# First attention of a two-block model laid out features by tokens, two heads per step, with its gates by tanh

## The reference, cut to what matters

```python
def first_block(x, ...):
    h = rms_norm(x, norm_mix_g[i])
    za_u, za_v, q, k, v_att, g_a, g_b = jnp.split(h @ w_in[i], offsets, axis=-1)   # 7 parts of 1024
    y_a = sgu_mixer(gelu(za_u), gelu(za_v), w_s, b_s, ln_g, ln_b)   # u * (tril(W_s) v + b) per chunk of 128 tokens
    y_b = moba_attention(heads(q), heads(k), heads(v_att), rel_bias)  # 16 heads of 64, causal over 256 tokens
    merged = jax.nn.sigmoid(g_a) * y_a + jax.nn.sigmoid(g_b) * y_b
    x = x + merged @ w_out[i]
    h = rms_norm(x, norm_ffn_g[i])
    x = x + jnp.square(jax.nn.relu(h @ w_ff1[i])) @ w_ff2[i]
    ...
```

## Time and profile before

| | us |
|---|---|
| median of 3 runs | 1606.94 (1603.93 to 1608.2) |
| profiled execution: its time, its span | 1607.9, 1605.6 |
| PE busy | 1497.6 (93%) |
| DVE busy, ACT busy | 554.0 (35%), 466.3 (29%) |

### The profile page before, as it was taken

How to read it: one execution, slowest core, us unless ns; L and a number is a source line. 1 busy time by engine, 2 the same in 40 slices (tenths; PEclk the granted TensorE clock), 3 DMA queues, 4 the chain that set the end, 5 groups by cost and what they waited for, 6 DMA issues and landing times.

```text
span 1605.6 us, 20677 instructions
## 1 busy us (share of the span) xinstructions
PE 1497.6 (93%) x7963; PEld 931.0 (58%) x7963; DVE 554.0 (35%) x862; ACT 466.3 (29%) x785; POOL 37.0 (2%) x42
## 2 busy tenths in 40 slices
PE   7999979999999999979999989889889899999996
PEld 6897869988889987744434324324334343444342
DVE  5754566654574767641111101101101111111112
ACT  5535635452463676321111101101101111111111
POOL 1000000000020000120000000000000000000000
PEclk9999989999999999899999999999999999999999
DMA  8464334545544321779999999999999999999996
GB/s 303 162 212 156 105 125 158 195 173 183 187 155 158 106 105 53 285 300 422 417 414 422 421 422 422 422 422 422 422 421 423 422 422 404 411 421 422 422 421 251
DMA packets 106930, 489.27 MB, mean 305 GB/s; under 512 B 9391, under 2 KB 11571, under 8 KB 60020
## 3 DMA queue, kind: packets, MB, share of 16 engines
q1 hardware_dynamic: 105604, 484.16, 76.0%
q0 software_dynamic: 1184, 4.26, 0.8%
q10 hardware_dynamic: 80, 0.02, 0.0%
HBM read 506.21 MB, written 1.08 MB: 316 GB/s over the span
## 4 chain that ended last, share of the span: by engine, by line
PE 55%; DMA 23%; DVE 5%; ACT 2%; issue 1%; SPq 1%; DVEq 0%; ACTq 0%
PE bank L980 20%; DMA slots<-in_w_up_dram 20%; PE bank L1419 18%; PE bank L1454 8%; DMA slots<-in_w_down_dram 3%; PE bank L1369 3%; PE bank L1379 2%; DVE w_split L1556 1%; ACT w_split L606 1%; SPq L435 1%; PE bank L970 1%; PE bank L1042 1%; DVE xeT L2067 0%; ACT h_hi L596 0%; PE bank L1050 0%
## 5 line engine op out<-in xcount | busy, mean ns | idle before, releaser
L1419 PE MATMUL bank<-slots,xeT 128*64 128x512 f32 x1536 | 354.7, 616 | 41.0 <-DMA slots<-in_w_up_dram 38.6
L1419 PEld LDWEIGHTS bank<-slots,xeT 128*64 128x64 f32 x1536 | 112.6, 141 | 278.5 <-issue 219.2
L1454 PE MATMUL bank<-slots,heT 128*64 128x512 f32 x1024 | 227.2, 595 | 9.5 <-ACT heT L909 7.5
L1556 DVE TENSOR_TENSOR w_split<-raw,w_split 128x2048 fp32r<-128x2048 f32 (+2 forms) x96 | 205.6, 2170 | 77.8 <-ACT w_split L606 77.6
L980 PE MATMUL bank<-w_split,h_hi 128*128 128x512 f32 (+1 forms) x672 | 211.6, 398 | 6.8 <-DVE h_lo L1546 3.9
L980 PE MATMUL bank<-h_hi,w_split 128*128 128x256 f32 x1120 | 208.0, 286 | 2.2 <-DVE w_split L1556 2.2
L606 ACT ACTIVATE w_split<-raw 128x2048 fp32r<-128x2048 f32 (+2 forms) x96 | 170.9, 1816 | 63.0 <-PE bank L980 56.4
L980 PEld LDWEIGHTS bank<-h_hi,w_split 128*128 128x128 f32 x1120 | 177.6, 194 | 3.8 <-DVE w_split L1556 2.6
L2076 DVE TENSOR_TENSOR h_e<-bank,h_e 128x512 f32<-128x512 f32 x32 | 22.1, 692 | 423.7 <-PE bank L1419 423.7
L980 PE MATMUL bank<-h_lo,w_split 128*128 128x256 f32 x560 | 159.5, 285 | 0.0
L1454 PEld LDWEIGHTS bank<-slots,heT 128*64 128x64 f32 x1024 | 70.7, 137 | 147.4 <-issue 130.1
(11 more groups left out here) (329 smaller groups left out, 1391.0 us busy)
## 6 DMA issues: line engine op xcount, KB each, us to landing
slots<-in_w_up_dram SPq DMA_DIRECT2D x128, 1024.0 KB
slots<-in_w_down_dram SPq DMA_DIRECT2D x128, 1024.0 KB
areas<-in_w_gate_dram SPq DMA_DIRECT2D x64, 1024.0 KB, 19.4
slots<-in_w_gate_dram SPq DMA_DIRECT2D x64, 1024.0 KB
raw<-in_w_in_dram SPq DMA_DIRECT2D x42, 1024.0 KB, 5.2
raw<-in_w_ff_dram SPq DMA_DIRECT2D x32, 1024.0 KB, 5.2
raw<-in_w_out_dram SPq DMA_DIRECT2D x12, 1024.0 KB, 5.0
raw<-in_w_ple_gate_dram SPq DMA_DIRECT2D x4, 1024.0 KB, 5.2
```

The lines of the kernel that those rows point to most:

```text
L1419: last = mm(bank[SLOTS * e:SLOTS * e + SLOTS, :], xeT[:, k, odd, SLOTS * e:SLOTS * e + SLOTS], expert_panel(w, e, odd)[:, k, :], start=(k ...
L1454: last = mm(banks[half][SLOTS * e:SLOTS * e + SLOTS, :], heT[:, c, SLOTS * e:SLOTS * e + SLOTS], expert_panel("down", e, odd)[:, c, 512 * ...
L1556: last = tt(lo, source, hi, ALU.subtract)
```

## The change

The gates, `u`, the attention's output and their merge are kept features by tokens, as q and k are. So the panels u, gb and ga take the column form; the SGU mix has `v_rows` as its stationary operand and gives features by tokens, its bias coming as a row broadcast over the partitions (`b_row`, a new DMA of 128x1024 behind the layer norm's two, and the small one of `b_sgu` is gone). A step holds the two heads of a 128-feature tile. The probabilities are scaled by DVE ahead of their transposes (`head_norm`), and the values matmuls have the 64 columns of `va` as stationary operand, write the two halves of bank 7's partitions, and give the transposed output; so `turn(T_MERGED)` goes. The sigmoids become `tanh(x/2)`, with the factor 0.5 applied as the merged tiles are rounded, and merging happens in three pieces (`merge`, `round_merged`, `split_merged`). The first three quarters of wo panel 0 move in among the last heads. In the diff the first loop over `KT` is ACT's, the second DVE's.

```diff
-           ("va", 0), ("va", 1), ("gb", 0), ("gb", 1), ("ga", 0), ("ga", 1), ("wo", 0), ("wo", 1)]
+           ("va", 0), ("va", 1), ("gb", 0), ("ga", 0), ("gb", 1), ("ga", 1), ("wo", 0), ("wo", 1)]
...
+                    sp.dma_start(b_row.rearrange("p g t -> p (g t)"),
+                                 b_sgu.rearrange("a g t -> a (g t)").to_broadcast([P, D])).then_inc(ln_loaded, 16)
...
-            pool.wait_ge(merged, MT)
+            pool.wait_ge(scores_taken, HEADS)
...
-                        ins = act_({"ga": sga, "gb": sgb}[kind][:, b, half], bank[:, :], ACT.Sigmoid)
+                        dst = {"ga": sgaT, "gb": sgbT}[kind][:, tiles, :]
+                        ins = act_(dst.rearrange("p k t -> p (k t)"), bank[:, :], ACT.Tanh, scale=0.5)
...
+            for j in range(KT):
+                if j:
+                    pair_turned(j - 1)
+                if j % 2:
+                    empty(*(("gb", 0), ("ga", 0), ("gb", 1), ("ga", 1))[j // 2])
+                head_exp(2 * j)
+                head_exp(2 * j + 1)
+                for q in SPLIT_BESIDE[j]:
+                    split(2 * AT["ga", 0] + q)
+                if j == 4:
+                    round_merged(1, 0, 4, 2)
+                if j == 7:
+                    round_merged(2, 4, 6, 1)
...
-                if kind in ("q", "k", "q2", "ff1", "xbc"):
+                if kind in ("u", "q", "k", "ga", "gb", "q2", "ff1", "xbc"):
...
+            def score_pair(j):
+
+                if j:
+                    pe.wait_ge(scores_taken, 2 * j)
+                rows = [slice(DH * e, DH * e + DH) for e in range(2)]
+                for e in range(2):
+                    mm(banks[4 + e][:, P:384], qT[rows[e], j, P:S], kT[rows[e], j, :], start=True, stop=True)
+                for e in range(2):
+                    mm(banks[4 + e][:, 0:P], qT[rows[e], j, 0:P], kT[rows[e], j, 0:P], start=True, stop=True).then_inc(scored, 1)
...
+            def values_pair(j):
+
+                pe.wait_ge(softT_ready, 2 * j + 2)
+                for m, tokens in ((0, slice(0, S)), (1, slice(P, S))):
+                    for e in range(2):
+                        last = mm(banks[7][DH * e:DH * e + DH, S + tokens.start:2 * S], va[:, m, DH * (2 * j + e):DH * (2 * j + e) + DH],
+                                  softT_flat[:, 384 * e + S * m:384 * e + S + P * m], start=(m == 0), stop=True,
+                                  skip_group_check=(m == 1))
+                last.then_inc(heads_out, 2)
...
-            banks_empty(AT["ga", 1])
-            pe.wait_ge(merged, 2)
-            turn(T_MERGED)
-            whole("wo", 0, T_MERGED)
+            score_pair(0)
+            whole("gb", 0)
+            beside = [(kind, j, c) for kind, j in (("ga", 0), ("gb", 1), ("ga", 1), ("wo", 0)) for c in range(4)]
+            for j in range(1, KT):
+                turn_pair(j - 1)
+                score_pair(j)
+                quarter(*beside[2 * j - 2])
+                values_pair(j - 1)
+                quarter(*beside[2 * j - 1])
+            turn_pair(KT - 1)
+            quarter("wo", 0, 2)
+            values_pair(KT - 1)
             quarter("wo", 1, 0)
             quarter("wo", 1, 1)
+            quarter("wo", 0, 3)
+            quarter("wo", 1, 2)
             banks_empty(AT["wo", 0])
             turn(T_FFN, (0, 1))
-            quarter("wo", 1, 2)
             quarter("wo", 1, 3)
...
+            for j in range(KT):
+                head_scores(2 * j)
+                head_scores(2 * j + 1)
+                if j == 7:
+                    gate_mixed(1)
+                head_norm(2 * j)
+                head_norm(2 * j + 1)
+                if j:
+                    gate_pair(j - 1)
+                if j == 3:
+                    gate_mixed(0)
+                if j == 4:
+                    merge(0, 4)
+                if j == 5:
+                    split_merged(0, 4, 2)
+                if j == 7:
+                    merge(4, 6)
+                    split_merged(4, 6, 1)
+                split(*(2 * AT["ga", 0] + q for q in SPLIT_BESIDE[j]))
+            gate_pair(KT - 1)
+            merge(6, 8)
+            split_merged(6, 8, 1)
```

More of the change, by code:

```diff
@@ L666, in head_exp, with pair_turned, round_merged @@
                 last.then_inc(probs_ready, 1)
+            def pair_turned(j):
+                act.wait_ge(probs_turned, 2 * j + 2)
+                if j:
+                    act.wait_ge(heads_out, 2 * j)
+                act_(softT_flat[:, 0:512], banks[6][:, :], ACT.Copy).then_inc(softT_ready, 1)
+                act_(softT_flat[:, 512:768], banks[7][:, 0:S], ACT.Copy).then_inc(softT_ready, 1)
+            def round_merged(n, first, last_one, groups):
+                act.wait_ge(merged, n)
+                act_(merged_hi[:, first:last_one, :], sgbT[:, first:last_one, :], ACT.Copy, scale=0.5).then_inc(hT_a, groups)
             def head_turned(n):
@@ L1087, in _ @@
             pe.wait_ge(line_copied, 1)
-            for m in range(MT):
-                for half in range(2):
-                    for g in range(4 * half, 4 * half + 4):
-                        last = mm(banks[4 + 2 * m + half][:, P * (g % 4):P * (g % 4) + P], w_sT[:, g, :],
-                                  v_rows[:, m, P * g:P * g + P], start=True, stop=True)
-                    last.then_inc(sgu_mixed, 1)
+            for i in range(4):
+                for g in (2 * i, 2 * i + 1):
+                    for m in range(MT):
+                        at = S * (g % 2) + P * m
+                        last = mm(banks[4 + i][:, at:at + P], v_rows[:, m, P * g:P * g + P], w_sT[:, g, :], start=True, stop=True)
+                last.then_inc(sgu_mixed, 1)
             for kind, j in (("k", 0), ("k", 1), ("va", 0), ("va", 1)):
@@ new lines, in gate_mixed, with merge @@
+            def gate_mixed(half):
+                dve.wait_ge(emptied_a, emptied("a", AT["ga", half]))
+                dve.wait_ge(ya_ready, 4)
+                tiles = slice(4 * half, 4 * half + 4)
+                flat = lambda v: v[:, tiles, :].rearrange("p k t -> p (k t)")
+                link(stt(flat(uT), flat(sgaT), 1.0, flat(uT), ALU.add, ALU.mult))
+            def merge(first, last_one):
+                dve.wait_ge(heads_kept, 2 * last_one)
+                tiles = slice(first, last_one)
+                tt(sgbT[:, tiles, :], sgbT[:, tiles, :], uT[:, tiles, :], ALU.add).then_inc(merged, 1)
@@ new lines, in split_merged, with head_output @@
+            def split_merged(first, last_one, groups):
+                dve.wait_ge(hT_a, 4 * T_MERGED + last_one // 2)
+                tiles = slice(first, last_one)
+                flat = lambda v: v[:, tiles, :].rearrange("p k t -> p (k t)")
+                stt(flat(merged_lo), flat(sgbT), 0.5, flat(merged_hi), ALU.mult, ALU.subtract).then_inc(hT_d, groups)
+            def head_output(n):
+                dve.wait_ge(probs_ready, n + 1)
+                link(tt(head_sum[:, n % 4, 0:2], head_sum[:, n % 4, 0:2], sink_e[:, n % 4, :], ALU.add))
+                recip(head_sum[:, n % 4, 2:4], head_sum[:, n % 4, 0:2]).then_inc(inverse_ready, 1)
@@ L1683, in _ @@
             dve.wait_ge(emptied_a, emptied("a", AT["u", 1]))
-            for m in range(MT):
-                for half in range(2):
-                    dve.wait_ge(sgu_mixed, 2 * m + half + 1)
-                    for g in range(4 * half, 4 * half + 4):
-                        u = u_rows[:, m, P * g:P * g + P]
-                        last = stt(u, banks[4 + 2 * m + half][:, P * (g % 4):P * (g % 4) + P], col("b_sgu", g), u,
-                                   ALU.add, ALU.mult)
-                    last.then_inc(ya_ready, 1)
+            for i in range(4):
+                dve.wait_ge(sgu_mixed, i + 1)
+                mixed, tiles = area(9)[:, 512 * i:512 * i + 512], slice(2 * i, 2 * i + 2)
+                link(tt(mixed.rearrange("p (g m t) -> p g m t", g=2, m=MT),
+                        banks[4 + i][:, :].rearrange("p (g m t) -> p g m t", g=2, m=MT),
+                        b_row[:, tiles, :].unsqueeze(2).to_broadcast([P, 2, MT, P]), ALU.add))
+                tt(uT[:, tiles, :], uT[:, tiles, :], mixed.rearrange("p (k t) -> p k t", k=2), ALU.mult).then_inc(ya_ready, 1)
             for kind in ("k", "va"):
@@ L1697, in _ @@
             dve.wait_ge(bias_loaded, 16)
-            def merge(half):
-                at = slice(512 * half, 512 * half + 512)
-                dve.wait_ge(emptied_a, emptied("a", AT["ga", half]))
-                dve.wait_ge(heads_kept, 8 * half + 8)
-                dve.wait_ge(ya_ready, 4)
-                tt(u_rows[:, :, at], u_rows[:, :, at], sga[:, :, at], ALU.mult)
-                link(tt(yb[:, :, at], yb[:, :, at], sgb[:, :, at], ALU.mult))
-                tt(yb[:, :, at], yb[:, :, at], u_rows[:, :, at], ALU.add).then_inc(merged, 1)
-            for step in range(HEADS + 2):
-                if step < HEADS:
-                    head_scores(step)
-                if step >= 2:
```

(14 more changed lines are left out.)

115 lines of the change are left out of this document (61 added, 54 removed).

## The result

The changed kernel takes 1581.95 us (median of 4 runs, 1580.82 to 1584.03); the kernel before takes 1605.43 (4 runs, 1602.27 to 1608.2, three of them those of the median 1606.94 in the table ahead of the change). The ratio is 0.9864, with an interval of 0.9851 to 0.9878. The forecast of 1590.0 with 1584 to 1599 around it was too high: the sign held and most terms of the sum did, the size did not. The profiled execution took 1581.83 us, its span is 1579.7.

A forecast was written before the change was run, and what follows sets the result against it. PE, gapless in the attention, was taken to bound that part, DMA the experts. Savings of 19.7 - 0.3 - 0.4 - 1.1 - 1.0 = 16.9 us took the profiled 1607.9 to 1591.0, median 1590.0, range 1584 to 1599.

The forecast's parts named there:

- Rounds without idle time on PE: Attention: eight rounds of two heads, 8.8 us apart on PE, with no idle time.
- whole gb 0: Weight panel gb 0 on PE, after the first scores: 11.52 + 0.12 = 11.64 us in column form.
- the quarters: Attention rounds on PE: two column-form quarters of a weight panel take 6.0 us per round.
- the transposes: Attention rounds on PE: the transposes of a pair of heads take 0.7 us.
- the clock at 1.00 through the stretch: PE's granted clock would stay at 1.0 throughout, where the drain behind the heads had 0.59 before.
- the drain's gaps gone: Behind the last heads: 8.24 us of PE idle gaps would vanish, part of the 19.7 us gain.
- the tail behind ff1's first matmul: Behind ff1's start: wo panels end closer together, DVE has more to do at once; costs 1.0 us.
- panel u 1 and its waits: Panel u 1 ahead of the attention: a 0.6 us wait plus 0.5 for column form, costing 1.1 us.
- The rival that DVE sets the pace: Attention rounds: DVE or ACT paces them, a pair takes 9.8 instead of 8.8 us, total 1597; chance 0.08.
- the overlap of the two heads: Pairs on PE share the array partly: scores 1.1 us (bounds 0.85 to 1.7), values 1.0 (0.8 to 1.3-1.4).
- The rival of full sharing: Pairs on PE overlap fully: scores 0.85, values 0.8, 3.6 us less, total 1586.4; chance 0.14.
- The stalls of 0.3 and 0.4 us around the last `w_out` quarters: PE waits 0.3 us in round 7 for merged data and 0.4 before ff1 for DVE.

The follow-up runs named there:

- e4: Changed kernel with the first three quarters of wo panel 0 put back behind the last values, nothing in their place; 1591.76 us.
- e5: Changed kernel with one unused DVE reduction of 1024 columns (1.22 us) added at the end of each round; 1587.95 us.
- e9: Changed kernel with both heads of a pair computing scores from the first head's row half, which alters the data; 1599.03 us.
- e13: Changed kernel with both heads of a pair writing values to the first head's column half, which alters the data; 1573.16 us.
- e7: Changed kernel run once more with no edit; 1581.61 us beside 1603.38 for the kernel before, ratio 0.9861.
- e8: Kernel before, run once more unedited to see where its low-clock places fall; traced span 1601.3 us.
- e14: Kernel before, run again unedited to time its stretch from the wait near 265 to the experts; traced span 1601.9 us.

## Why the prediction was wrong

**The steps that held.** Rounds without idle time on PE; whole gb 0 in 150.08 - 138.47 = 11.61 (forecast 11.64); the quarters 3.07 + 2.97 (6.0); the transposes 0.74 (0.7); the clock at 1.00 through the stretch; the drain's gaps gone (e4 puts 8.4 us on this); the tail behind ff1's first matmul 16.58 against 15.38, 1.2 dearer (1.0); panel u 1 and its waits, from its first matmul to the first scores 137.62 - 52.91 = 84.71 us against 136.75 - 53.33 = 83.42, 1.3 dearer (1.1). The rival that DVE sets the pace didn't come about, but 1.2 us more a round already cost 3.9 in all (e5).

**The step that failed: the overlap of the two heads.** The forecast let the second head's matmuls start only behind the first head's second, "so in a run of eight short ones about one is exposed; I take 1.1", and 1.0 for the values. Measured 0.86 and 0.80, my own lower bounds: (0.24 + 0.20) x 8 = 3.5 us. I had two bounds that were both worked out from rows, and a row of two tiles side by side at full rate, and put the value between them by a thought about order that no row showed. The rival of full sharing, with its 3.6 us, was what the rows bore out and got 0.14. e9 and e13 show the mechanism and its price without it. The trace of before could have told: in the experts, where the program gives both instructions of one tile ahead of the other's, a short window has

```profile
1003.60 0.60 PE L1419 MATMUL bank<-slots,xeT 128*64 128x512 f32 x2
```

so the first instructions of both column halves start together there too, and none is exposed.

**Smaller terms.** The stalls of 0.3 and 0.4 us around the last `w_out` quarters didn't come: the window 208.98 to 228.30 has 0.12 of gaps. That is 0.6 us cheaper than forecast; the transposes and quarters were 0.6 dearer over eight rounds. Together: 94.0 was forecast to ff1's first matmul, 90.68 came, 3.3 less.

**The rest.** The forecast was a saving of 16.9 us; the medians say 23.5 in the first comparison, and 1603.38 - 1581.61 = 21.8 in that of e7. Stretch A gives 128.37 - 107.3 = 21.1 and panel u 1 takes 1.3 of it back. What is over, 3.7 us in the first comparison and 2.0 in that of e7, lies in code that the change doesn't touch, and some of it in which executions were compared: the kernel before had medians of 1603.38, 1603.48 and 1603.93 in three sets of 7 to 9 runs and 1605.43 in the 4 beside the result, so the base that I forecast from, 1606.94, was 1.5 above the last. My range had no term for that. With sharing in full and the base of 1605.43 my own sum would have given 1605.43 - 16.9 - 3.6 = 1584.9, still 3 over the result, and inside my range. Of the 8.0 us between forecast and result the overlap is thus 3.5, the base 1.5, and the remaining 3.0 stay without a shown cause.

## What to carry to other kernels

Where two matmuls of half the rows or half the columns stand next to each other, price them at full sharing once the trace shows any pair of halves doing it, and keep the other bound for the range. In a software pipeline, fill the last iteration too: 8.4 of the 21.1 us in stretch A come from three quarters of the next weights that stand among the last heads, between a softmax and its use. And compare stages between fixed instructions: a stretch repeated to 0.1 us here, while whole executions scattered by 2 to 4, and three kernels with altered data were up to 12 us off in a stage that they didn't touch.

## What the runs showed of the hardware

- Two fp32 matmul groups on separate row halves take 0.86 us against 1.51 in one half, on separate column halves of one PSUM bank 0.80 against 1.44: factors of 1.76 and 1.80, with the first and last matmul of a group included.
- A program order by head ran as if it were interleaved (151.40, 151.72, 151.93 above), and the experts' tiles did so in the kernel before (two at 1003.60).
- The first long products, at 13.8 to 14.2 us, took 1.22 us a pair in some executions and 0.73 in others, and for 4 us all products took nearly twice as long in the former: 1.22, 0.63 and 1.05 in the first trace of the changed kernel, the durations of e4 from 212.42 on at a granted clock of 0.50. The windows say 1.00 for that time in both, but there they rest on nothing: the trace's clock records begin at 17.78 us in the one and at 13.48 in e7's, and the products turn fast at 17.80. The same kernel then has its first scores at 137.62 and at 135.92. Among traces with 1.22 they come at 136.68 to 137.04 before the change and at 137.62 to 138.36 behind it. e8 has 0.73 there, but a granted clock of 0.50 from 50.85 to 54.26, from the end of PE's wait of 2.28 us ahead of u 1 on, which costs it 1.5 us (84.88 from u 1 to the first scores, against 83.42).
- Stretches of 3 to 10 us with a granted clock of 0.50 (1.2 GHz) fall into work that keeps PE busy too, some us behind a wait: in the first trace of before from 523.75 on, with PE busy 7.42 of the 8 us from 523 to 531, behind a wait of 1.31 us ahead of 517.73. The same wait in e14 (ahead of 517.70) is followed by none.
